# Rounding of normalised activations moved from VectorE to ScalarE ahead of three projections

## What is computed

```
h = rms_norm(x, norm_g)                 # x * rsqrt(mean(x^2) + eps) * g
...
def conv_ffn(x, norm_g, w_up, conv_w, conv_b, w_down):
    h = rms_norm(x, norm_g)
    u = causal_dwconv(h @ w_up, conv_w, conv_b)      # 3 taps
    gate, val = jnp.split(u, 2, axis=-1)
    return x + (jax.nn.silu(gate) * val) @ w_down

# layer 0: even mixer, conv_ffn;  layer 1: qkv = rms_norm(x, g) @ w_qkv, attention, conv_ffn
```

## Time and profile before

| | |
|---|---|
| median of three runs | 1741.36 us (1732.87 to 1741.48) |
| profiled execution | 1736.12 us, its span 1734.3 us |
| TensorE busy | 1608.8 us, 93% |
| VectorE busy | 716.8 us, 41% |
| ScalarE busy | 511.7 us, 30% |
| GpSimd busy | 110.2 us, 6% |

### The profile page before, as it was taken

The page is one execution under the profiler, slowest core; times in us unless marked ns, Lnnn a source line. Parts: engine busy times, 40 slices in busy tenths (PEclk is TensorE's granted clock), DMA queues, the critical chain, the costliest instruction groups (busy, mean ns, idle before and its releaser), DMA issues.

```text
span 1734.3 us, 28065 instructions
## 1 busy us (share of the span) xinstructions
PE 1608.8 (93%) x10788; PEld 1277.3 (74%) x10788; DVE 716.8 (41%) x1412; ACT 511.7 (30%) x809; POOL 110.2 (6%) x47
## 2 busy tenths in 40 slices
PE   7957899989998999989998887998999999999998
PEld 5627899989957999978887876787555555555554
DVE  1963888638574788322432521311411111111112
ACT  2124455443353556342214103301211111111111
POOL 0000112212101222200000000000000000000000
PEclk9968899998998999989999987999799999999999
DMA  8752355664433655614533211243899999999993
GB/s 312 271 200 73 122 169 162 192 228 132 136 122 122 181 181 181 185 48 134 155 114 95 61 49 32 93 155 112 347 407 414 417 415 415 412 418 412 413 418 154
DMA packets 57803, 375.52 MB, mean 217 GB/s; under 512 B 6416, under 2 KB 6672, under 8 KB 42128
## 3 DMA queue, kind: packets, MB, share of 16 engines
q1 hardware_dynamic: 57744, 374.69, 58.9%
HBM read 373.61 MB, written 1.05 MB: 216 GB/s over the span
## 4 chain that ended last, share of the span: by engine, by line
PE 75%; issue 19%; DVE 3%; ACT 3%; POOL 0%; POOLq 0%; DVEq 0%; ACTq 0%
PE lin L598 14%; PE mixp L1102 6%; PE mixp L1106 6%; PE stat L1128 6%; PE lin L579 5%; PE lin L580 4%; PE lin L581 4%; PE lin L1082 4%; PE stat L1068 4%; PE lin L856 2%; PE stat L1074 1%; PE stat L579 1%; PE mixp L581 1%; PE mixp L580 1%; PE mixp L579 1%
## 5 line engine op out<-in xcount | busy, mean ns | idle before, releaser
L579 PE MATMUL lin<-r_hi,w_hi 128*128 128x256 f32 x1024 | 305.6, 298 | 29.2 <-DVE r_lo L1500 16.6
L580 PE MATMUL lin<-r_lo,w_hi 128*128 128x256 f32 x1024 | 296.3, 289 | 0.0
L581 PE MATMUL lin<-r_hi,w_lo 128*128 128x256 f32 x1024 | 296.1, 289 | 0.0
L598 PE MATMUL lin<-h,ring 128*128 128x256 f32 x1280 | 287.1, 384 | 3.0 <-DVE h L1512 3.0
L598 PEld LDWEIGHTS lin<-h,ring 128*128 128x128 f32 x1280 | 244.5, 192 | 42.6 <-issue 9.4
L579 PEld LDWEIGHTS lin<-r_hi,w_hi 128*128 128x128 f32 x1024 | 202.9, 198 | 36.9 <-issue 15.8
L580 PEld LDWEIGHTS lin<-r_lo,w_hi 128*128 128x128 f32 x1024 | 203.6, 199 | 0.7
L581 PEld LDWEIGHTS lin<-r_hi,w_lo 128*128 128x128 f32 x1024 | 203.2, 198 | 0.0
L1482 DVE TENSOR_TENSOR w_lo<-ring,w_hi 128x1024 fp32r<-128x1024 f32 x129 | 160.1, 1246 | 91.8 <-ACT w_hi L1176 70.5
L1102 PE MATMUL mixp<-arena 128*64 128x256 f32 x1024 | 154.0, 379 | 0.0
L1106 PE MATMUL mixp<-arena 128*64 128x256 f32 x1024 | 153.9, 379 | 0.0
(11 more groups left out here) (365 smaller groups left out, 2216.2 us busy)
## 6 DMA issues: line engine op xcount, KB each, us to landing
arena<-in_experts SPq DMA_DIRECT2D x96, 2048.0 KB, 11.1
ring<-in_panels SPq DMA_DIRECT2D x272, 512.0 KB, 3.6
aring<-in_ada SPq DMA_DIRECT2D x24, 1024.0 KB, 6.0
cst<-in_consts SPq DMA_DIRECT2D x1, 1696.0 KB, 11.8
x<-in_x SPq DMA_DIRECT2D x1, 1024.0 KB, 4.8
out_x<-x SPq DMA_DIRECT2D x2, 512.0 KB, 2.6
rows<-in_rows SPq DMA_DIRECT2D x1, 542.0 KB, 12.9
mixers<-in_even_w_s SPq DMA_DIRECT2D x1, 512.0 KB, 13.6
```

The source lines that it names most:

```text
L579: pe.matmul(o, w_hi[:, slot, c], r[0], start=start, stop=False, skip_group_check=True)
L580: pe.matmul(o, w_hi[:, slot, c], r[1], start=False, stop=False, skip_group_check=True)
L581: return pe.matmul(o, w_lo[:, slot, c], r[0], start=False, stop=stop, skip_group_check=True)
L598: mm = pe.matmul(lin[b][:, 0:T], w[:, i, :], rhs[:, i, :], start=i == 0, stop=i == k - 1)
```

## The change

ScalarE gets a helper, `round_rows`: for each of the eight tiles it waits for VectorE's normalise and copies the tile into `r_hi`. `stream_norm` calls it after the norm and ahead of the next weight panels, except at the three norms that `split_stream` does not serve (the first one, the one ahead of the second block and the one ahead of the experts), where `rows=False`. VectorE's `split_stream` normalises and subtracts; its subtraction waits for ScalarE's rounding.

```
+            def round_rows():
+
+                for k in range(KD):
+                    act.wait_ge(h_whole, seen(h_whole))
+                    act.activation(r_hi[:, k, :], h[:, k, :], ACT.Copy).then_inc(r_hi_ready, 1)
+
-            def stream_norm(first=False, down=False):
+            def stream_norm(first=False, down=False, rows=True):
...
                 norm_rest(1, D)
+                if rows:
+                    round_rows()
                 if not first:
                     split_hi(panels.n + 4)
...
                 dve.wait_ge(rs_ready, seen(rs_ready))
-                at = {}
                 for k in range(KD + 2):
                     if k < KD:
                         dve.scalar_tensor_tensor(h[:, k, :], x[:, k, :], gain(k), rs[:, 0, :], ALU.mult, ALU.mult)\
-                            .then_inc(dve_step, 1)
-                        at["whole", k] = seen(dve_step)
-                    if 1 <= k <= KD:
-                        dve.wait_ge(dve_step, at["whole", k - 1])
-                        dve.tensor_copy(r_hi[:, k - 1, :], h[:, k - 1, :]).then_inc(dve_step, 1)
-                        at["hi", k - 1] = seen(dve_step)
+                            .then_inc(h_whole, 1)
                     if k >= 2:
-                        dve.wait_ge(dve_step, at["hi", k - 2])
+                        dve.wait_ge(r_hi_ready, seen(r_hi_ready))
                         dve.tensor_tensor(r_lo[:, k - 2, :], h[:, k - 2, :], r_hi[:, k - 2, :].bitcast(F32), ALU.subtract)\
                             .then_inc(h_ready, 1)
```

More of the change, by code:

```diff
@@ L252, in program @@
         h_ready = sem("h_ready")
+        h_whole = sem("h_whole")
+        r_hi_ready = sem("r_hi_ready")
         dve_step = sem("dve_step")
@@ L1241, in _ @@
             act.wait_ge(consts_loaded, 48)
-            stream_norm(first=True)
+            stream_norm(first=True, rows=False)
             act.activation(c_act[:, :], col("c", 0, KD), ACT.Silu).then_inc(silu_done, 1)
@@ L1314, in conv_tiles @@
                 panels.advance(count)
-            stream_norm(down=True)
+            stream_norm(down=True, rows=False)
             for m in range(KD):
@@ L1414, in _ @@
             gates(1, 0, 12)
-            stream_norm()
+            stream_norm(rows=False)
             shifted(1)
```

## The result

| | before | changed |
|---|---|---|
| median | 1733.98 us (9 runs, 1731.22 to 1741.48) | 1725.33 us (9 runs, 1722.23 to 1727.49) |
| ratio | | 0.9944, 95% interval 0.9926 to 0.9963 |
| span of the profiled execution | 1734.3 us | 1723.5 us |
| VectorE, ScalarE busy | 716.8, 511.7 us | 710.6, 521.9 us |

Two things went wrong: the size of the gain, and the time from which I subtracted it.

The account below looks back on a forecast made before the run. TensorE, waiting for and slowly fed by VectorE's row work at three stages, was taken as the bound; 3 x 1.0 + 2.35 = 5.35 us off 1741.36 gave 1736.0 us, range 1727 to 1743.

Parts of the forecast that it names:

- First subtraction, pace, roundings hidden: Each edited stage: first subtraction at 1.20 us, a tile every 0.74, ScalarE's 0.42 roundings hidden two tiles behind.
- What that is worth: Earlier start and fewer first-panel holes gain 1.0 us per stage (bounds 0.8 to 1.45), 3.0 for three stages.
- The stall's 2.35 us: Ahead of the first FFN: GpSimd's subtraction, moved to 7.4, no longer blocks VectorE's normalise; worth 2.35 us.
- What is late next: After the first panel: later weight panels, table load and first tap cost nothing; weight margins of 4 us and more.
- The first FFN's gain reaches the end: First FFN's loop: its cycle starts earlier by what the second panel gains, so the gain is carried whole.
- The long cycle: First FFN's loop: four panels still take 12.6 us, against 11.5 in the second FFN.
- neither rival: Second FFN falls into the first's cycle, 5.35 us slower, chance 0.05; first FFN leaves it, 15.0 faster, chance 0.09.
- The handoff rival: Wait on ScalarE costs 0.5 us more, first subtraction 0.36 later three times; 1.1 us less gain, 1737.1; chance 0.10.
- my own 5.35: Whole kernel: the forecast gain in us, 3 x 1.0 for the stages plus 2.35 for the first FFN's stall.

Follow-up runs that it names:

- extra_cast: Changed kernel with a cast of each normalised tile into an unused buffer put back on VectorE where its rounding stood; ratio to before 1.0004.
- weights_first: Changed kernel with ScalarE's two orders exchanged: the two weight panels first, then the eight roundings; ratio to before 0.9935.
- hold_weights: Kernel before, but ahead of the first FFN ScalarE holds its two weight panels until VectorE's fifth subtraction is done; ratio to before 0.9999.
- first_only: Changed kernel with ScalarE rounding only ahead of the first FFN; qkv and the second FFN as in the kernel before; ratio to before 0.9966.
- slot2: Changed kernel with GpSimd's slot of the ring changed from 3 to 2; ratio to before 0.9935.
- late_start: Kernel before, but TensorE waits, ahead of each tile of the first panel, for three subtractions more (up to the eighth); ratio to before 1.0017.

## Why the prediction was wrong

**First subtraction, pace, roundings hidden: right.** 1.19 and 0.74 against 1.20 and 0.74, a rounding of 0.42, restart at 1.76.

**"What that is worth": the step that failed.** I let the half-clock stretch last as long after the restart as before, 8.6 us, and so gave a stage 1.0 us, with 1.45 as the bound. The return came after 3.8 to 5.9 us instead. Against extra_cast, which differs by the holes and the start alone, the second panel's result is earlier by 2.3, 2.9 and 2.2 us, each above my bound, 7.3 us in all of the some 10 that the timed runs show. The kernel before could not have shown this: all its stages had holes. I had taken the return for a property of the restart, where the runs show that it depends on how closely the products follow: weights_first restarts 0.50 us later than the kernel before and is back at full clock some 2 to 4 us sooner all the same. The early start and the lost holes are 1.45 us of it; the rest is products run at 0.12 instead of 0.213 us. In the timed runs half clock lasted 143 us in the changed kernel and 161 before (mean clock 0.9586 over 9 runs, 0.9537 over 71). 18 us less, of which up to 8 us would be saved time, since a product at half clock takes 0.213 for 0.12, a loss of 0.44 us in each us that TensorE works at half clock. In profiles the three returns together are 10.0 us shorter in the changed kernel than in extra_cast, and 14.3 and 8.5 us shorter than in the two profiles of the kernel before; where the rest of the 18 comes from is not shown. In profiles, attention had 3 to 10 us of half clock with no pattern by kernel.

**The stall's 2.35 us: the mechanism right, its worth open.** GpSimd starts at 7.35 after the first normalise, as forecast (7.4), and the normalise is at its 0.48. In profiles the removal is worth 1.5 to 2.7 us. In timed runs hold_weights shows 0.2 us (a loss of 2.3 to a gain of 2.4), and extra_cast no gain either. I cannot say why the two differ.

**"What is late next": one thing cost something.** Weight panels were in time. But ScalarE's first tap, late behind weight copies and table load (t = 8.69 with the first panel done at about 7.2), holds back the first FFN's VectorE: its first silu (row 186.53 above) waits 0.95 us for VectorE. That silu starts at t = 11.88 in the changed kernel, in first_only and in slot2 alike, though their second panels come at 10.4, 10.7 and 10.2, so VectorE and not TensorE sets it. Of the 4.98 us won at the second panel, 4.41 are left at qkv (214.51 to 210.10). I had said that nothing is lost and the gain is carried whole.

**The first FFN's gain reaches the end: right**, but for these 0.57 us. The long cycle stayed at 12.6 us in the changed kernel, and the second FFN at 11.52; neither rival happened.

**The handoff rival: wrong.** ScalarE's first rounding starts 0.04 after its tile's normalise ended, and no subtraction waits.

**The time from which I subtracted.** I took the median of three runs, 1741.36, though the profiled execution was at 1736.12. 71 further runs have a mean of 1735.4, and only 6 of them lie above 1740; of my three runs two did. From 1735.4 my own 5.35 would have given 1730.1, inside my range; so would the measured 9.7 us from 1741.36, 1731.7. It took both errors to leave it.

## What to carry to other kernels

Where TensorE restarts after a pause at half clock, holes between its first products were paid twice here: as holes, and as a later return to full clock. Look at the first panel after each pause for an engine that feeds it slower than TensorE takes it (here 0.93 us per tile against 0.64), and take instructions off that engine; but keep the start early: a dense start 0.5 us later still gained (weights_first), one 2.8 us later gained nothing (late_start). And compare equal loops by their cycle: where the same loop takes 12.59 in one place and 11.52 in another, the place of one GpSimd instruction in it can be worth about as much as the edit at hand (0.9944 to 0.9889 here).

## What the runs showed of the hardware

- TensorE's return to full clock (2.4 GHz) from 1.2 GHz after a pause: 6.9 to 8.8 us after the restart where a tile of 0.64 us of products came each 0.93 us (15 stages, pauses of 4.5 to 5.1 us), 3.8 to 6.6 us where it came each 0.74 us or without holes (24 stages, pauses of 4.1 to 9.9 us). The Trainium skill (TensorE: Matmul & The Clock Gate, What's actually happening) says that the clock follows how busy TensorE has been, and that a kernel's cold stretch varies from run to run; the trace agrees with both, and where its products came with holes the return was later in every one of these stages.
- Executions of one kernel differ by their granted clock: before, runs at 1731 us had 0.956 and runs at 1741 us 0.949 to 0.951.
- GpSimd's subtraction of 2.4 us held up VectorE instructions with both inputs in SBUF: a normalise (2.57 instead of 0.48), a subtraction (2.36 instead of 0.41).
